# Moving the first small loads of a two-block transformer kernel to other queues, and one weight split ahead of the position tables

## The reference

```python
def rms_norm(x, gain):
    xf = x.astype(jnp.float32)
    y = xf * lax.rsqrt(jnp.mean(xf * xf, axis=-1, keepdims=True) + RMS_EPS)
    return (y * gain.astype(jnp.float32)).astype(x.dtype)

def diff_attention(h, pos, w_qkv, q_gain, k_gain, ..., rel_table, lam_init):
    qkv = h @ w_qkv                      # h is rms_norm(x, attn_norm[0]): 256 x 1024, w_qkv 1024 x 3072
    ...
        bucket = t5_bucket(p_blk[:, :, None] - pos[:, None, :])
        bias = jnp.take(rel_table, bucket, axis=0).astype(f32)
    ...
```

## Time and profile before

| | us |
|---|---|
| median of 3 runs | 1316.03 (1315.77 to 1316.54) |
| the profiled execution | 1318.53 |
| its span, first to last instruction | 1316.8 |
| mean granted TensorE clock | 0.995 |
| TensorE / VectorE / ScalarE / GpSimd busy | 1261.5 / 882.3 / 689.8 / 365.5 |

### The profile page before, as it was taken

How to read it: one execution, slowest core, us unless ns; L and a number is a source line. 1 busy time by engine, 2 the same in 40 slices (tenths; PEclk the granted TensorE clock), 3 DMA queues, 4 the chain that set the end, 5 groups by cost and what they waited for, 6 DMA issues and landing times.

```text
span 1316.8 us, 24171 instructions
## 1 busy us (share of the span) xinstructions
PE 1261.5 (96%) x8884; PEld 1092.2 (83%) x8884; DVE 882.3 (67%) x1388; ACT 689.8 (52%) x1217; POOL 365.5 (28%) x377
## 2 busy tenths in 40 slices
PE   6999999999999999999999999999989999999996
PEld 5887899999998877898999998888755699987666
DVE  7868688666668985558966666753377548453674
ACT  5555455454467777545545446544367515413562
POOL 4951244434321140244443432011012220000022
PEclk9999999999999999999999999999999999999998
DMA  8565247666645542255666654422200364532100
GB/s 311 177 238 176 81 145 259 204 235 228 208 143 161 175 128 81 78 189 181 211 242 208 229 200 132 133 75 95 94 1 1 71 170 144 161 97 80 49 1 33
DMA packets 50505, 191.72 MB, mean 146 GB/s; under 512 B 5936, under 2 KB 6320, under 8 KB 48112
## 3 DMA queue, kind: packets, MB, share of 16 engines
q1 hardware_dynamic: 43632, 158.59, 36.9%
q0 software_dynamic: 6064, 31.33, 6.8%
q10 hardware_dynamic: 720, 0.57, 0.2%
HBM read 189.41 MB, written 1.05 MB: 145 GB/s over the span
## 4 chain that ended last, share of the span: by engine, by line
PE 80%; DVE 8%; ACT 7%; issue 3%; POOL 1%; DMA 1%; DVEq 0%; SPq 0%; ACTq 0%; POOLq 0%
PE G L416 14%; PE G L418 13%; PE G L417 13%; PE A L416 6%; PE A L418 6%; PE A L417 6%; PE R L636 3%; DVE WL L1126 3%; PE R L562 2%; ACT WH L1823 2%; PE R L416 1%; PE R L418 1%; PE R L417 1%; PE A L994 1%; PE G L1003 1%
## 5 line engine op out<-in xcount | busy, mean ns | idle before, releaser
L1126 DVE TENSOR_TENSOR WL<-RAW,WH 128x1024 fp32r<-128x1024 f32 x295 | 381.5, 1300 | 289.6 <-ACT WH L1823 289.3
L1823 ACT ACTIVATE WH<-RAW 128x1024 fp32r<-128x1024 f32 x295 | 310.3, 1057 | 414.8 <-PE G L418 302.9
L416 PE MATMUL G<-XH,WH 128*128 128x256 f32 (+1 forms) x1336 | 400.3, 300 | 9.5 <-DVE WL L1126 6.2
L417 PE MATMUL G<-XL,WH 128*128 128x256 f32 (+1 forms) x1336 | 395.0, 296 | 0.0
L418 PE MATMUL G<-XH,WL 128*128 128x256 f32 (+1 forms) x1336 | 395.0, 296 | 0.0
L416 PEld LDWEIGHTS G<-XH,WH 128*128 128x128 f32 x1336 | 255.6, 191 | 33.0 <-issue 25.7
L417 PEld LDWEIGHTS G<-XL,WH 128*128 128x128 f32 x1336 | 255.8, 191 | 6.3
L418 PEld LDWEIGHTS G<-XH,WL 128*128 128x128 f32 x1336 | 255.6, 191 | 6.3
L416 PE MATMUL A<-HH,WH 128*128 128x256 f32 x352 | 101.0, 287 | 3.7 <-POOL HL L2440 3.7
L417 PE MATMUL A<-HL,WH 128*128 128x256 f32 x352 | 100.9, 287 | 0.0
L418 PE MATMUL A<-HH,WL 128*128 128x256 f32 x352 | 100.8, 286 | 0.0
(11 more groups left out here) (345 smaller groups left out, 2364.2 us busy)
## 6 DMA issues: line engine op xcount, KB each, us to landing
RAW<-in_wst SPq DMA_DIRECT2D x295, 512.0 KB, 3.8
M<-in_wmod POOLq DMA_DIRECT2D x16, 1024.0 KB, 6.6
M<-in_wmod POOLq DMA_DIRECT2D x16, 512.0 KB, 6.5
B<-in_rpb POOLq DMA_DIRECT2D x4, 1024.0 KB, 11.7
H<-in_x_t SPq DMA_DIRECT2D x2, 512.0 KB, 7.5
M<-in_x_tok SPq DMA_DIRECT2D x1, 1024.0 KB, 11.0
M<-in_ctx_t POOLq DMA_DIRECT2D x1, 1024.0 KB, 5.3
out_y<-M SPq DMA_DIRECT2D x2, 384.0 KB, 2.7
```

The costliest lines, as they stand in the source:

```text
L416: mm(out, lh, rh, start=start, stop=False, skip_group_check=True)
L417: mm(out, lh, rl, start=False, stop=False, skip_group_check=True)
L1126: v.tensor_tensor(WL[:, slot, :], RAW[:, raw, :], WH[:, slot, :].bitcast(F32), ALU.subtract).then_inc(w_lo, 1)
L1823: act(WH[:, slot, :], RAW[:, raw, :], ACT.Copy).then_inc(w_hi, 1)
```

## The change

The gains of the first layer (4 KB) are loaded from ScalarE's queue instead of SyncE's, ahead of all else on ScalarE. SyncE so issues the first half of x directly behind panel 0. Positions, keys, table and the lambda vectors are loaded from GpSimd's queue instead of ScalarE's, when the first half of x has landed. On VectorE the low part of panel 3 is issued behind the threshold add, ahead of the table of differences; the add now signals its own semaphore, `t_key`, for which VectorE waits again behind the table work, and GpSimd's step rows wait for it instead of `t_tab`.

```diff
@@ -78,6 +78,7 @@
     VC[_name] = _n
     _n += _m
 NV = _n
+GAINS = VC["attn0"] + KD
 
 
 CCOLS = [("ident", 128), ("ones", 128), ("blk", 128), ("rot", 128), ("rot2", 128), ("clear", 128), ("causal", 128), ("nbm", 64),
@@ -332,7 +333,7 @@
         fin_sq, out_g, out_p = sem("fin_sq"), sem("out_g"), sem("out_p")
         nb_ok, small_ok, out_t, y_out = sem("nb_ok"), sem("small_ok"), sem("out_t"), sem("y_out")
         ao_x = sem("ao_x")
-        in_gain = sem("in_gain")
+        in_gain, t_key = sem("in_gain"), sem("t_key")
         in_x2, in_xt, x_sq = sem("in_x2"), sem("in_xt"), sem("x_sq")
 
 
@@ -378,16 +379,14 @@
                     sp.wait_ge(w_lo, freed)
                 sp.dma_start(RAW[:, slot, :], w_ap[p]).then_inc(w_raw[slot], 16)
 
-            gains = VC["attn0"] + KD
             panel(0, 0, None)
-            sp.dma_start(V[:, 0:gains], vec[:, 0:gains]).then_inc(in_gain, 16)
             sp.dma_start(H[:, 0:4, :], x_t[:, 0:4, :]).then_inc(in_x, 16)
             panel(1, 1, None)
             sp.dma_start(H[:, 4:8, :], x_t[:, 4:8, :]).then_inc(in_x2, 16)
             panel(2, 2, None)
             panel(3, 3, None)
             sp.dma_start(XTOK, x_tok).then_inc(in_xt, 16)
-            sp.dma_start(V[:, gains:NV], vec[:, gains:NV]).then_inc(in_vec, 16)
+            sp.dma_start(V[:, GAINS:NV], vec[:, GAINS:NV]).then_inc(in_vec, 16)
             panel(4, 4, None)
             panel(5, 5, None)
             sp.dma_start(C[:, :], cst).then_inc(in_cst, 16)
@@ -1229,7 +1228,8 @@
             dv.wait_ge(in_tab, 48)
             link(v.tensor_copy(POSF, POSI.bitcast(I32)))
             link(v.tensor_copy(KEYF, KEYI.bitcast(I32)))
-            link(v.tensor_scalar(TKEY, KEYF, THR, None, ALU.add))
+            v.tensor_scalar(TKEY, KEYF, THR, None, ALU.add).then_inc(t_key, 1)
+            ahead(1)
             link(v.tensor_tensor(TD, TAB3, PREV3, ALU.subtract))
             for i in range(3):
                 link(v.tensor_copy(THI, TD))
@@ -1240,6 +1240,7 @@
                     link(v.tensor_copy(TD, TREST))
             v.memset(SM[:, 32:33], 0.0).then_inc(t_tab, 1)
 
+            dv.wait_ge(t_key, 1)
             made = [0]
 
             def steps_of_first(n):
@@ -1899,11 +1900,9 @@
             def arrived(k):
                 ac.wait_ge(in_x if k < 4 else in_x2, 16)
 
+            ac.dma_start(V[:, 0:GAINS], vec[:, 0:GAINS]).then_inc(in_gain, 16)
             ac.wait_ge(small_ok, 1)
             load_table(ACT.Sqrt)
-            ac.dma_start(POSI.bitcast(I32), pos.broadcast_to([P, T])).then_inc(in_tab, 16)
-            ac.dma_start(KEYI.bitcast(I32), pos4).then_inc(in_tab, 16)
-            ac.dma_start(TAB, tab).then_inc(in_tab, 16)
             split_hi(0, 0, 0, 16)
             ac.wait_ge(in_gain, 16)
             x_high(H, "attn0", 0, 4, arrived)
@@ -1911,7 +1910,6 @@
             nxt[0] = 2
             x_high(H, "attn0", 0, KD, arrived, None, 4)
             ahead(0)
-            ac.dma_start(LAMV, lam4.broadcast_to([P, T])).then_inc(in_lam, 16)
             ac.wait_ge(in_vec, 16)
 
             def first_use():
@@ -2400,7 +2398,12 @@
             def always(i):
                 pass
 
-            gp.wait_ge(t_tab, 1)
+            gp.wait_ge(in_x, 16)
+            gp.dma_start(POSI.bitcast(I32), pos.broadcast_to([P, T])).then_inc(in_tab, 16)
+            gp.dma_start(KEYI.bitcast(I32), pos4).then_inc(in_tab, 16)
+            gp.dma_start(TAB, tab).then_inc(in_tab, 16)
+            gp.dma_start(LAMV, lam4.broadcast_to([P, T])).then_inc(in_lam, 16)
+            gp.wait_ge(t_key, 1)
             for c in range(1, 4):
                 for j in range(16):
                     n = 16 * c + j
```

## The result

The changed kernel takes 1320.96 us (median of 7 runs, 1319.20 to 1321.89), the kernel before 1316.03 (7 runs, 1315.16 to 1317.69): ratio 1.0031, 95% interval 1.0022 to 1.0041. By the ratio that is 4.1 us slower (2.9 to 5.4); the difference of the two medians is 4.9. The profiled execution took 1320.58, its span is 1318.9.

What follows compares the result with a forecast made beforehand. VectorE, without idle from 15.07 to about 46, was taken to make TensorE late: 18.77 plus 6.61 plus 1.5 slowing gives 26.88, matmul 26.98 instead of 24.02, so 1316.0 + 3.0 = 1319.0; range 1315.0 to 1322.0.

Steps and rivals of the forecast that it cites:

- A: Likeliest case: VectorE's queue makes TensorE 3.0 us later at panel 4, giving 1319.0 (own range 1317.5 to 1320.5); chance 0.42.
- B: Rival: TensorE's clock also falls behind a stall of over 5 us, six matmuls costing 1.3 more, 1320.3; chance 0.20.
- x and the start: First half of x lands at 6.4 instead of 8.43, TensorE starts at about 7.7 instead of 9.77; worth nothing by itself.
- The vectors: Rest of the vectors, awaited by ScalarE for panel 3's high part, lands 0.5 earlier, at 16.55 instead of 17.05.
- C: Rival: vectors land 1.9 earlier, at 15.15, and tables don't feel GpSimd: no change, 1316.1; chance 0.28, 0.05 a real gain.
- Panel 3: VectorE's low part runs 17.64 to 18.77, so TensorE gets panel 3 at 18.9, 2.3 us earlier.
- The table beside GpSimd: Eleven small VectorE table operations, now beside GpSimd's step rows, slow by 0.14 each, 1.5 us; bounds 0 and 3.4.
- VectorE's queue: Behind panel 3: table and gains 2.69, six step rows 2.71, panel 4's low part 1.21, together 6.61 without slowing.
- Nothing gives it back: VectorE stays fully loaded behind panel 4 and TensorE sets the pace from about 46, so the 3.0 stays lost.
- D: Rival: the table, issued third on GpSimd, lands late, at worst 19.8: +6.0, 1322.0; decides at 16.8; chance 0.10.
- GpSimd's earlier end: GpSimd ends its step rows earlier than before, but no TensorE wait in this part is for them.

Runs made afterwards that it cites:

- e2: Changed kernel with VectorE's order and GpSimd's wait as before, so only the loads are moved: 1317.36 against 1317.33 for the kernel before, 0.9997.
- e6: Changed kernel, but GpSimd's step rows wait for the end of the tables again: 1320.52 against 1316.38 for the kernel before, 1.0036.
- e3: Changed kernel with 30 more matmuls filling TensorE's stall between panels 3 and 4: 1318.69, 1.0011 of the kernel before.
- e1: Kernel before with only VectorE's order changed, panel 3's low part right behind the threshold add: 1319.79 against 1317.33, 1.0022.
- e5: Changed kernel with VectorE's six step rows behind panel 4's low part instead of in front: 1319.28 against 1316.38 for the kernel before, 1.0020.
- e11: e7 with panel 3's low part ahead of the casts, no step rows before panels 4 and 5, six rows moved later: 1314.51 against 1317.22, 0.9983.
- e4: Changed kernel, but ScalarE waits for the rest of the vectors only ahead of its second unit: 1320.58 against 1317.33 for the kernel before, 1.0027.
- e7: e4 with GpSimd's large loads held until TensorE's fifth unit is nearly through: 1317.19 against 1316.38 for the kernel before, 1.0006.
- e9: Changed kernel with only GpSimd's large loads held until TensorE's fifth unit is nearly through: 1320.34 against 1317.22 for the kernel before, 1.0023.
- e10: Changed kernel measured again, word for word, beside e9: 1322.70 (5 runs), 1.0040 of the kernel before.

## Why the prediction was right, and where it was not

The likeliest case, A, gave +3.0 and 1319.0; measured were +4.1 (2.9 to 5.4) and 1320.96. That is inside the stated range (to 1322.0), but 0.5 above A's own (to 1320.5), and nearest to B's 1320.3. The mechanism is A's, with B's on top, and a third that no case had.

- **x and the start.** Forecast 6.4 for x and 7.7 for the first matmul; measured 6.8 (1.31 + 5.5) and 8.13. Beside the earlier issue I had taken 1.6 off x's landing, where rows 5 have 1.01 of idle; 1.2 came. That TensorE's start is worth nothing by itself held (e2). A detail was off: panels 0 to 2 took 10.4 instead of 9.76, since TensorE had nine slow matmuls at its start instead of six.
- **The vectors.** Forecast 16.55, measured 16.35, 0.7 before 17.05. C needed 15.1. Most of what x gained in rows 5 did not reach them.
- **Panel 3.** Low part forecast 17.64 to 18.77, measured 17.45 to 18.6; TensorE at 18.77 instead of 18.9. But it was still busy to 18.56, so the stall before panel 3 was 0.21 and not 1.4.
- **The table beside GpSimd: the term that was mis-sized.** Forecast 1.5 for eleven operations, measured 0.3 (2.62 against 2.32). Only the three casts feel GpSimd, 0.08 each (e6 shows it); the eight others are unchanged. The last 0.06 is the new wait for `t_key` in front of the gains (e6, with short casts, still has 2.38), which the prediction put at nothing. I had taken one mean for all kinds of operation, from shapes of another line. None waited out a whole step row, which is what the Trainium skill's "SBUF — State Buffer", section on the two physically separate sides, would have with its lock that blocks the loser to the end. That section names among the VectorE operations that take the lock those with two inputs in SBUF; here the two-input TENSOR_TENSOR are among the unchanged (0.16 to 0.19). The measurement decides.
- **VectorE's queue.** Table and gains 2.99 with the 0.3 (forecast 2.69 without), six rows 2.53 to the next start (2.71), low part 1.21. The sum ended at 26.88 by forecast and at 25.32 (24.11 + 1.21) in truth, first matmul into R 25.46 instead of 26.98: +1.44 instead of +3.0. Of the 1.56, 1.2 is the table, 0.2 the vectors, 0.2 the rows.
- **Nothing gives it back.** Held but for 0.3: the shift was +3.13 from panel 6 to 62 us and +2.86 at 76.
- **B, the clock.** Forecast 1.3 at a chance of 0.20 for a stall of over 5 us; it came true at a stall of 3.71, with 1.69. e3 shows the cause, e1 repeats it (1.72). The warning of the Trainium skill, "TensorE: Matmul & The Clock Gate", table of recommendations, that a long idle gap between bursts brings the lower clock back, agrees with the falls behind 3.50 to 3.71, and I gave it too little weight. I had also written that no stall in the trace before was long enough to show it; that was misread, for the same trace has the fall behind the stall of 1.85 at 373 us.
- **D** did not come: the table landed at 15.03, 6.6 after its issue; it would have had to be 16.8.
- **The second loss** was in no case. I had written that GpSimd's earlier end costs nobody, since no TensorE wait is for its rows. What the early end triggers, six large loads 4 us sooner, I did not follow.

So A's +3.0 is met by the first loss (+3.13) only by luck, by two errors that cancel: 1.56 too much in the stall, 1.7 left out behind it. What is above that in the profile, 1.9 near 83 us, was not foreseen at all.

## What to carry to other kernels

When an operation is pulled forward on an engine that has no idle time, add up what is still queued in front of the next one that the critical engine needs: here panel 3 came 2.4 us earlier and panel 4 1.4 later. Ask of every engine that gets done sooner which transfers it will then start, and what else must pass through the DMA engines at that time, perhaps instructions too. And a stall of TensorE is not to be counted by its length alone: one stall of 3.7 cost 1.7 more through the clock, while e5's four of 1.24 or less cost only their own length; where the work can't be made less, move its deadline, as e11 does.

## What the runs showed of the hardware

- Stalls of 1.73 and 2.16 before panel 4 (e4, e7) and of 2.38 before panel 3 (e2) left TensorE at its 2.4 GHz level, those of 3.50 to 3.71 before panel 4 (e1, e6, e9, e10, changed) were all followed by the 1.2 GHz one. The price varied between executions of one kernel: seven matmuls 0.43 apart, or 12. At 83 us the fall came in all three executions with a stop (0.56, 0.57 and 1.77, within tiny matmuls) and in none without, and at 373 us it came in five of 13 executions behind the same stall of 1.85. Length alone doesn't decide it.
- With the DMA engines full, TensorE stood still at one fixed instruction until 2.35 to 2.52 us after the start of the window with the instruction queue's packet, three times out of three (changed, e4, e5). That it starved for instructions is the likely reading, not a shown one; e7 shows that holding the large loads back takes the stop away.
- Beside GpSimd's rows a 128x8 cast to bfloat16 takes 0.25 instead of 0.17, a 128x8 subtraction or a copy the same 0.17 (changed and before; e6 has the cast at 0.17 again).
